# Gathers of expert rows on GpSimd: loops with copied indices and register waits, or a straight program that reads the indices in place

## What is computed

```python
# 8 heads, top 16 of 128 x 128 experts; u_tab, v_tab: 16384 x 2048
eidx = take_along_axis(cidx, pos)          # (token, 8, 16)
g = softmax(top)
u, v = u_tab[eidx], v_tab[eidx]
a = gelu(einsum('thkd,td->thk', u, xb))    # dots
out = einsum('thk,thkd->td', g * a, v)     # weighted sums
```

## Time and profile before

| | us |
|---|---|
| median of 3 runs | 2883.98 |
| lowest, highest | 2883.62, 2892.7 |
| span of the profiled execution | 2896.9 |
| its busy time: VectorE, GpSimd | 1865.8, 1475.1 |

### The profile page before, as it was taken

The page is one execution under the profiler, slowest core; times in us unless marked ns, Lnnn a source line. Parts: engine busy times, 40 slices in busy tenths (PEclk is TensorE's granted clock), DMA queues, the critical chain, the costliest instruction groups (busy, mean ns, idle before and its releaser), DMA issues.

```text
span 2896.9 us, 19315 instructions
## 1 busy us (share of the span) xinstructions
PE 1325.8 (46%) x5913; PEld 1008.8 (35%) x5913; DVE 1865.8 (64%) x2673; ACT 216.5 (7%) x539; POOL 1475.1 (51%) x989
## 2 busy tenths in 40 slices
PE   8999998778899999999500000000000000000000
PEld 7886776545587862888400000000000000000000
DVE  4105556476111041135999998999988888888887
ACT  1001111133100010020000000000000000000000
POOL 2005666360200000001487668668688888888885
PEclk9999998778899999999755555555555555555555
DMA  8434322231334448436698889889898989999997
GB/s 326 145 107 167 112 96 114 87 93 59 116 138 148 151 162 324 152 131 260 256 416 359 367 344 389 343 332 376 321 392 355 377 358 376 380 384 394 355 391 311
DMA packets 107284, 757.87 MB, mean 262 GB/s; under 512 B 12952, under 2 KB 12984, under 8 KB 17800
## 3 DMA queue, kind: packets, MB, share of 16 engines
q0 software_dynamic: 82720, 582.35, 50.9%
q1 hardware_dynamic: 24496, 174.66, 16.7%
HBM read 748.67 MB, written 12.48 MB: 263 GB/s over the span
## 4 chain that ended last, share of the span: by engine, by line
PE 40%; DVE 23%; POOL 16%; issue 11%; DMA 8%; ACT 1%; DVEq 0%; POOLq 0%; SPq 0%; ACTq 0%
PE bank L335 14%; DVE sb_mv_n L1933 9%; POOL sb_ring L1864 6%; PE bank L324 5%; POOL sb_m_t L1864 4%; PE bank L670 4%; PE bank L663 4%; POOL sb_mk_t L1864 4%; DMA sb_mk_t<-in_peer_u,sb_z_t 2%; PE bank L1357 2%; DVE sb_ring L1924 2%; DMA sb_ring<-in_peer_v,sb_z_t 2%; DMA sb_ring<-in_peer_u,sb_z_t 1%; DVE sb_m_t L1924 1%; POOL sb_z_t L1883 1%
## 5 line engine op out<-in xcount | busy, mean ns | idle before, releaser
L1864 POOL DMA_INDIRECT sb_ring<-in_peer_v,sb_z_t x132 | 285.6, 2164 | 100.2 <-DVE sb_mv_n L1933 44.7
L1933 DVE SCALAR_TENSOR_TENSOR sb_mv_n<-sb_ring,sb_h_t,sb_mv_n 128x2048 f32<-128x2048 f32 x128 | 301.6, 2356 | 51.6 <-DMA sb_ring<-in_peer_v,sb_z_t 36.9
L1864 POOL DMA_INDIRECT sb_ring<-in_peer_u,sb_z_t x124 | 264.2, 2131 | 118.7 <-DVE sb_ring L1924 66.8
L1924 DVE SCALAR_TENSOR_TENSOR sb_ring<-sb_ring,sb_y_t 128x2048 f32<-128x2048 f32 x120 | 271.4, 2291 | 37.2 <-DMA sb_ring<-in_peer_u,sb_z_t 35.6
L1825 PE MATMUL bank<-sb_h_t,sb_con 8*128 8x128 f32 x2 | 0.8, 482 | 599.8 <-DVE sb_h_t L1801 599.8
L335 PE MATMUL bank<-sb_x_t,sb_ring 128*128 128x264 f32 x1024 | 228.2, 387 | 0.0
L1870 POOL COPY sb_z_t<-sb_z_t 128x8 int32<-128x8 int32 x6 | 4.7, 788 | 429.4 <-DVE sb_z_t L1793 427.4
L1825 PEld LDWEIGHTS bank<-sb_h_t,sb_con 8*128 8x128 f32 x2 | 0.5, 305 | 600.1 <-issue 600.1
L335 PEld LDWEIGHTS bank<-sb_x_t,sb_ring 128*128 128x128 f32 x1024 | 195.1, 191 | 32.7
L1864 POOL DMA_INDIRECT sb_m_t<-in_peer_u,sb_z_t x70 | 147.4, 2106 | 55.1 <-DVE sb_m_t L1916 35.0
L335 PE MATMUL bank<-sb_y_t,sb_ring 128*128 128x264 f32 x768 | 171.2, 387 | 0.0
(11 more groups left out here) (414 smaller groups left out, 2915.7 us busy)
## 6 DMA issues: line engine op xcount, KB each, us to landing
sb_ring<-in_w_z SPq DMA_DIRECT2D x28, 1024.0 KB, 4.8
sb_ring<-in_w_xk SPq DMA_DIRECT2D x16, 1024.0 KB, 4.8
sb_ring<-in_w_xv SPq DMA_DIRECT2D x16, 1024.0 KB, 5.2
sb_ring<-in_w_out SPq DMA_DIRECT2D x16, 1024.0 KB, 4.7
sb_ring<-in_w_xq SPq DMA_DIRECT2D x16, 1024.0 KB, 4.7
sb_ring<-in_mem_k SPq DMA_DIRECT2D x16, 1024.0 KB, 4.8
sb_ring<-in_mem_v SPq DMA_DIRECT2D x16, 1024.0 KB, 6.4
sb_ring<-in_w_xo SPq DMA_DIRECT2D x16, 1024.0 KB, 4.8
```

The source lines that it names most:

```text
L1864: pool.indirect_dma_start(SLOT[slot], None, A[table], bass.IndirectOffsetOnAxis(IXS[half][:, k:k + 1], 0))\
L1924: dve.scalar_tensor_tensor(out=SLOT[k], in0=SLOT[k], scalar=1.0, in1=XN[blk], op0=ALU.mult, op1=ALU.mult, accum_out=ACTV[:, bass.ds(i * NS ...
L1933: dve.scalar_tensor_tensor(out=HN[blk], in0=SLOT[k], scalar=WGT[blk][:, bass.ds(i * NSLOT + k, 1)], in1=HN[blk], op0=ALU.mult, op1=ALU.add ...
```

## The change

The program of GpSimd for the gathers becomes straight code: no loop, no registers, every wait on a constant. `IXS` is gone; each gather takes its column of indices straight from `EIX` or `EXS`. With it go the 66 copies and the waits on `ixs`. The waits on `peer_used` are on the same counts as before. For gathers 32 to 127 of block 0 the one wait for retrieval part 3 becomes a wait for each part ahead of its 32 gathers. The order of the gathers, their slots and all other engines stay as they are.

```diff
--- before.py
+++ after.py
@@ -1585,7 +1585,6 @@
         EXF, EXS = z_t[:, 6528:6536], z_t[:, 6864:6872].bitcast(I32)
         WS, AS, RED, STAT = z_t[:, 6536:6544], z_t[:, 6544:6552], z_t[:, 6552:6568], z_t[:, 6568:6592]
         KEYS = z_t[:, 6592:6848].rearrange("p (c n) -> p c n", c=2)
-        IXS = [z_t[:, 6848 + 8 * i:6856 + 8 * i].bitcast(I32) for i in range(2)]
         EXPW = z_t[:, 6880:7008]
 
         def pe_by_rows(pe):
@@ -1856,58 +1855,38 @@
 
         def pool_peer(pool):
 
-            with pool.register("round") as rnd, pool.register("use") as use:
-                pool.reg_mov(rnd, 1 + 4)
-                pool.reg_mov(use, 1 + 3 * NSLOT)
-
-                def gather(table, half, k, slot):
-                    pool.indirect_dma_start(SLOT[slot], None, A[table], bass.IndirectOffsetOnAxis(IXS[half][:, k:k + 1], 0))\
-                        .then_inc(S(f"slot{slot}"), 16)
-
-                def single(table, g, index, early=False):
-
-                    half = g // NSLOT % 2
-                    pool.tensor_copy(IXS[half], index).then_inc(S("ixs"), 1)
-                    pool.wait_ge(S("ixs"), g // NSLOT + 1)
-                    for k in range(NSLOT):
-                        if early and g + k >= 4:
-                            pool.wait_ge(S("peer_used"), g + k - 3)
-                        elif not early and (g > EARLY or k >= 4):
-                            pool.wait_ge(S("peer_used"), g + k + 1 - NSLOT)
-                        gather(table, half, k, 4 + k % 4 if early else k)
-
-                def gathers(table, blk, i0=0):
-
-                    with pool.Fori(i0, SLOTS // (2 * NSLOT)) as i:
-                        for half in range(2):
-                            pool.tensor_copy(IXS[half], EIX[blk][:, bass.ds(i * (2 * NSLOT) + half * NSLOT, NSLOT)])\
-                                .then_inc(S("ixs"), 1)
-                            pool.wait_ge(S("ixs"), rnd)
-                            pool.reg_add(rnd, rnd, 1)
-                            for k in range(NSLOT):
-                                pool.wait_ge(S("peer_used"), use)
-                                pool.reg_add(use, use, 1)
-                                gather(table, half, k, k)
-
-
-                pool.wait_ge(S("tk"), marks(2)[2])
-                pool.wait_ge(S("m_stored"), 32)
-                for g in range(0, EARLY, NSLOT):
-                    single("peer_u", g, EIX[0][:, g:g + NSLOT], early=True)
-                pool.wait_ge(S("tile"), tiles_before["pq"] + 16)
-                for g in range(EARLY, 2 * EARLY, NSLOT):
-                    single("peer_u", g, EIX[0][:, g:g + NSLOT])
-                pool.wait_ge(S("tk"), RETRIEVAL[3][3] + marks(2)[2])
-                gathers("peer_u", 0, 2)
-                gathers("peer_v", 0)
-                pool.wait_ge(S("ex_dve"), 7)
-                single("peer_u", U_S, EXS)
-                single("peer_v", V_S, EXS)
-                pool.reg_add(rnd, rnd, 2)
-                pool.reg_add(use, use, 2 * NSLOT)
-                pool.wait_ge(S("tk"), SECOND + marks(PH)[2])
-                gathers("peer_u", 1)
-                gathers("peer_v", 1)
+            def gather(table, index, g, slot, uses):
+                if uses:
+                    pool.wait_ge(S("peer_used"), uses)
+                pool.indirect_dma_start(SLOT[slot], None, A[table], bass.IndirectOffsetOnAxis(index, 0))\
+                    .then_inc(S(f"slot{slot}"), 16)
+
+            def gathers(table, blk, g0, lo=0, hi=SLOTS):
+
+                for n in range(lo, hi):
+                    g = g0 + n
+                    gather(table, EIX[blk][:, n:n + 1], g, g % NSLOT, g + 1 - NSLOT if g > EARLY or g % NSLOT >= 4 else 0)
+
+            def samples(table, g0):
+                for k in range(PH):
+                    gather(table, EXS[:, k:k + 1], g0 + k, k, g0 + k + 1 - NSLOT)
+
+            pool.wait_ge(S("tk"), marks(2)[2])
+            pool.wait_ge(S("m_stored"), 32)
+            for g in range(EARLY):
+                gather("peer_u", EIX[0][:, g:g + 1], g, 4 + g % 4, max(g - 3, 0))
+            pool.wait_ge(S("tile"), tiles_before["pq"] + 16)
+            gathers("peer_u", 0, U_OF[0], EARLY, 2 * EARLY)
+            for q in range(1, PARTS):
+                pool.wait_ge(S("tk"), RETRIEVAL[q][3] + marks(2)[2])
+                gathers("peer_u", 0, U_OF[0], q * 2 * TOPK, (q + 1) * 2 * TOPK)
+            gathers("peer_v", 0, V_OF[0])
+            pool.wait_ge(S("ex_dve"), 7)
+            samples("peer_u", U_S)
+            samples("peer_v", V_S)
+            pool.wait_ge(S("tk"), SECOND + marks(PH)[2])
+            gathers("peer_u", 1, U_OF[1])
+            gathers("peer_v", 1, V_OF[1])
 
         def dve_early_dots(dve, lo, hi):
             for g in range(lo, hi):
```

## The result

| us | before | after |
|---|---|---|
| median (runs) | 2883.93 (4) | 2819.01 (4) |
| lowest, highest | 2883.62, 2892.7 | 2817.15, 2820.89 |
| span of the profiled execution | 2896.9 | 2818.3 |
| ratio, 95% interval | | 0.9768 [0.975, 0.9785] |

The kernel is 64.9 us faster by the medians; 71 were forecast. First the page of the kernel after: its engine line, the DMA line in 40 slices with the line of GB/s under it, and the two instruction queues. They answer to the earlier trace rows.

A forecast was written before the change was run, and what follows sets the result against it. Vector engine bounds block 0's dots; in block 1 GpSimd loses a turn per round to index copies. 5 + 4 + 30 + 32 = 71 us off the 2896.9 span gives 2826, less 12.9 for the median: 2813 us, range 2795 to 2853 (0.78).

The forecast's parts named there:

- The bound: Block 0's dots: vector engine, nothing to gain; block 1: GpSimd one turn short per round, 22.5 us for eight gathers.
- The copy needs a turn of its own, so a round is nine turns for eight gathers: GpSimd beside vector operations in block 1: each index copy takes one 2.5 us turn, making rounds 22.5 us.
- theory G: Expectation for e9 and e3, not the prediction: whatever GpSimd has at the port in a gap between vector operations gets through.
- Sums of block 1: −32: Sums of block 1: eight turns for eight gathers, 128 x 2.50 = 320 us against 352.3, minus 32.
- Dots of block 1: −30: Dots of block 1: 2.45 us per dot by the transfers, two disturbances staying; 327 us against 357.2, minus 30.
- Two lock-outs stay: Starts of dots 1 to 64 and 65 to 128, block 1: long gathers remain, first ten dots costing 29.4 us each time.
- Sums of block 0 −5, samples −4: Waits removed by a better supplied ring in block 0's sums, 5 us, and waits on V rows in the samples, 4 us.
- Straight code, index in place: 0: GpSimd's gathers: indices read in place and registers made constants, hidden by the turn, and added instruction fetches: 0 us taken.
- Transfers bound already: Block 1: transfers already limit, ceiling 395 GB/s, 2.65 us per gather: 2854 us, chance 0.08; stages unchanged, 2875 us, 0.04.
- Lock-outs multiply: Block 1: vector engine runs through all landed rows each time, shutting GpSimd out; 789 us against 709.5, total 2955, chance 0.04.
- Fetches that cost up to 40 us: GpSimd's straight code: instruction fetches stall it, losing up to 40 of the 71 us; 2853 us, chance 0.06.
- GpSimd now waiting for the vector engine (slots full): Sign of being right, named with the rounds of block 1: GpSimd waits for the vector engine because all slots are full.

The follow-up runs named there:

- e2: Kernel after plus one index copy per round that no gather reads or waits for; only the next round's copy waits on it: 2834.82 us, ratio 0.981.
- e3: Kernel after plus two idle copies per round, one right behind the other, nobody waiting for them: 2890.77 us, ratio 1.0012.
- e4: Kernel before with its loops and registers, copies out; loop gathers read fixed index columns, the same 16 slots over and over: 2820.36 us, ratio 0.9758.
- e9: Kernel after with 12 register additions on GpSimd ahead of the first gather of each round, no copy: 2820.72 us, ratio 0.9766.
- e0: Kernel before, unchanged, run again for a second profile: 2888.95 us, profiled span 2886.8.
- e6: e5 with block 1's gathers fetching 4 KB rows instead of 8 KB and its dots multiplying by 0.0: 2811.27 us, ratio 0.9733.
- e11: Kernel after with block 1's gathers fetching 4 KB rows instead of 8 KB and its dots multiplying by 0.0: 2787.64 us, ratio 0.9647.
- e8: Kernel after, unchanged, run again in the second batch: 2818.0 us, ratio 0.9762.
- e5: Kernel after with a wait ahead of each dot of block 1 for the release of the dot before: 2808.57 us, ratio 0.9728.
- e7: Kernel after with the tokens of block 0 and block 1 exchanged in their tile: 2818.74 us, ratio 0.9762.
- e1: Kernel after with the 66 index copies and the waits on them put back, the rest straight and on constants: 2876.3 us, ratio 0.9955.

## Why the prediction was right, and where not

**The bound** was read rightly. That block 0's dots would give nothing (304.4 to 303.0), and that the vector engine's waits in block 1 came from GpSimd falling one turn short per round, both stand. So do nearly all signs named ahead (20.0 us per round, waits near zero in the sums); GB/s above 410 came in the sums (414) but not in the dots (400 over the stage, with the two long gathers in it).

**The copy needs a turn of its own, so a round is nine turns for eight gathers.** The arithmetic held (22.5 to 20.0 us), the reason did not. By e2 and e3 the copy rides in a gap and shares it with whatever comes at once behind it. The turn was lost by the gather that came 0.86 us late, a number that stood in my own rows and that I priced at zero: of registers and constants I wrote that "the turn hides it: 0". That holds for gather behind gather (e4, e9), not for the one behind a wait on a copy. In one batch, the way from before to after goes in three steps: straight code with constants 13.0 us (2889.3 to 2876.3), gathers that read the indices in place, so that nobody waits for the copy, 41.5 (to 2834.8), no copy at all 14.5 (to e4's 2820.4). The first step is not split further: loop, registers and the waits by quarters went together in it, and e4 shows only that loops and registers are free where no copy stands before them.

What the traces show of turns: in the sums of block 1 of the kernel after, 121 of the 122 recorded gathers take 2.18 to 2.20 us, and all 122 end 0.81 or 0.82 us behind the end of a vector operation (not the 0.7 of the text ahead); the shortest gather takes 0.93. A copy took 0.20 us where the vector engine was idle (at 2157.14 and 2367.17 in the kernel before) and 1.78 beside the sums. Dots and sums have two SBUF inputs. Beside an operation with one, a reduction over 128x2048 at 1679.24 (L1788, 2.29 us), a copy that started 0.78 us into it took 0.20; a gather that started 1.09 us into the reduction of the samples at 2032.78 (L1788, 8x2048, 2.27 us) took 0.94. At the edge of a sum, one that came 0.18 us into it took 3.01 (e3), and one whose start is recorded 0.06 us into it still came through at 0.96 (e2). Whether recorded starts are exact to 0.06 us no run here tells. The port of my rival and of theory G is a picture: the traces show these times and no port.

**Sums of block 1: −32**, measured −32.6 in the profiled pair and −33.2 against e0. The sum's 2.50 us is the vector engine's: half rows left it at 325.6 (e6, e11).

**Dots of block 1: −30.** Against the profiled execution −32.6, stage 324.6 where 327 was forecast. But in that execution the stage was longer than in the other profile of the same kernel: e0 has 348.9, and there the second long gather is 6.56 us, not 10.98. Against e0 the stage gives 22 to 24 us, so this term was 6 to 8 too large; the sums of block 0 and the samples, together 13.3 against e0 where 9 was forecast, make up 4 of it. All stages together give 71 against e0 (0.8, 13.3, 23.9, 33.2), and 77.5 against the execution profiled first. So the sum was 6.5 short of the execution that it was worked out on and 6 above the gain of the medians, off which I took it in full: that the forecast lies so near is in part luck.

The 6 us between 2813 and 2819.01 are not more than the batches differ: the gain was 68.9 us in the first (e4, which keeps the loops), 70.7 in the second (e8), 65.5 in the third (e9). The pace within the stage, 2.45 us by the transfers, was right, and e11 shows the cause. The rate that I put beside it did not fit: 1.049 MB in 2.45 us is 428 GB/s, not the 419 that I read over 54 us, and 428 is what came out over 114 and 120 us.

**Two lock-outs stay**: right, with 16.02 and 13.21 us. What winning them back would bring, 12 in the low end of my range, is 9.4 by e5. My reason was wrong in part. I wrote that the operations ran "back to back without letting GpSimd in"; a gap behind each dot does cure it (e5), but in e11, with dots 2.21 us apart without any gap, 114 of the 125 recorded gathers took 1.9 us, and two were long. What sets the starts of the halves apart, where the gather arrives with all slots landed, no run here tells. That stays open; e7 only rules out the operand's place.

**Sums of block 0 −5, samples −4**: −5.9 and −5.0. **Straight code, index in place: 0**: right; e4, with loops, took 2820.36 and the kernel after 2819.01. Queue 14 carried 31 instruction packets in the kernel before and in e0, 32 in e4, 34 or 35 in every kernel of straight code, about the four more that I had guessed. What one of them costs, and whether GpSimd waits for one, no run shows: the 40 us, and with them "through fetches" in the high end of the range and the 5 us for the loop's own work in the low end, were estimates. Measured is that from 2163 to 2808 us in the kernel after no idle time of GpSimd ahead of a gather that nothing explains is longer than 0.31 us, the usual gap.

**The rivals.** Transfers bound already: out by the −32.6 and −32.6; 428 GB/s came for 120 us on end where that rival had a ceiling of 395, though in the dots the transfers are the bound now. That rival also speaks of a page's limit: no run shows one, only these 428 GB/s. Lock-outs multiply: out, two stay. Fetches that cost up to 40 us: out, by the time of e4 and by the 0.31 us.

**The sign that did not come**: "GpSimd now waiting for the vector engine (slots full)". Even in e5, where the vector engine never waits for a row in block 1, no such idle time is recorded ahead of the gathers (0.30 us, by nothing that shows, ahead of nearly all). A gather's wait for its turn lies inside its recorded time, 2.14 us in the dots of e5 and 2.19 in the sums, against 0.93 for the shortest: nearly all of them end 0.81 us behind a vector operation's end. A full ring shows in the vector engine's missing waits.

## What to carry to other kernels

Beside back-to-back vector operations with two SBUF inputs, a GpSimd instruction got through here in its short time only near the gap between two of them (a gather in 0.96 us at 0.06 us into a sum, in 3.01 at 0.18), so what cost was not its length but whether it was there in time: take out waits between short GpSimd instructions and the next one (delay 0.16 us in e2, 0.27 with a wait in e1, 0.88 with register work and a loop besides in the kernel before). Where the vector engine runs without gaps and GpSimd feeds it, a wait that opens a 0.14 us gap per operation can pay (9.4 us here) if the stage is bound elsewhere anyway. Take a forecast's stage lengths from more than one execution: one stage differed by 9 us between two profiles of the same kernel. And count an instruction that slips through as a success only if its neighbour was running; beside an idle one it proves nothing.

## What the runs showed of the hardware that I had not expected

- One extra GpSimd copy that adds 0.12 us, read by nobody, cost 56 us in 66 rounds (e2 to e3, by medians of two batches), 30 of them in the sums of block 1. It moves the gather behind it from 0.06 to 0.18 us into the next vector operation, and the gather from 0.96 to 3.01 us.
- Twelve register additions ahead of a GpSimd instruction cost nothing measurable (e9: ratio 0.9766, the kernel after 0.9768), while between e1 and the kernel before, where a loop and a few register instructions stand behind the wait on a copy, the delay goes from 0.27 us to 0.87.
- Of the 24 gathers over 5 us in all profiles (6.6 to 16.1 us), 21 end some 0.8 us after the vector engine has run out of landed rows. The other three end sooner, among them the second of the kernel after, 0.88 us into the last landed dot. A gap of 0.14 us behind each dot makes them 2.98 and 4.35 us (e5). Gapless dots alone do not cause them (e11).
- Indirect gathers of 8 KB rows ran at 428 GB/s for 120 us with every DMA engine busy (share 1.01).
